# A two-layer hybrid encoder: the middle of the mixer in another order, and two of its masked copies moved from VectorE to ScalarE

## What is computed

```python
def hybrid_layer(x, ...):
    x = x + 0.5 * swiglu_ffn(rms_norm(x, ffn1_norm), ...)
    proj = rms_norm(x, mix_norm) @ w_in
    y_hy = hyena_mixer(hy_in, ...)     # two long convolutions, by DFT
    y_mla = mla_mixer(cq, ckv, kr, ...) # attention, 4 heads, rope on part of q and k
    y_gla = gla_mixer(q, k, v, gf, gb, r, ...) # gated linear attention, both directions
    x = x + concatenate([y_hy, y_mla, y_gla], -1) @ w_out
    return x + 0.5 * swiglu_ffn(rms_norm(x, ffn2_norm), ...)

def mla_mixer(...):
    q = (rms_norm(cq_in, q_norm) @ w_uq).reshape(B, S, MLA_HEADS, dqk)
    q = jnp.concatenate([q[..., :128], rope(q[..., 128:], pos)], axis=-1)
    s = jnp.einsum('bqhd,bkhd->bhqk', q_blk, k) * scale
    p = jax.nn.softmax(s, axis=-1)
    o = jnp.einsum('bhqk,bkhe->bqhe', p, v)      # then rms_norm(o, out_norm)

def gla_chunk_scan(q, k, v, g, inclusive):
    # o[i] = sum over j <= i (j > i in the backward direction) of
    #        (q[i] * exp(sum of g between j and i)) . k[j] * v[j]
```

## Time and profile before

| | |
|---|---|
| median of 3 runs | 1030.2 us (1030.1 to 1030.58) |
| the profiled execution | 1030.28 us |
| its span, first to last instruction | 1028.3 us |
| PE busy | 1001.0 us (97%) |
| DVE busy | 694.3 us (68%) |
| ACT busy | 537.3 us (52%) |
| POOL busy | 110.9 us (11%) |
| mean granted TensorE clock | 0.996 |

### The profile page before, as it was taken

How to read it: one execution, slowest core, us unless ns; L and a number is a source line. 1 busy time by engine, 2 the same in 40 slices (tenths; PEclk the granted TensorE clock), 3 DMA queues, 4 the chain that set the end, 5 groups by cost and what they waited for, 6 DMA issues and landing times.

```text
span 1028.3 us, 14899 instructions
## 1 busy us (share of the span) xinstructions
PE 1001.0 (97%) x5596; PEld 846.5 (82%) x5596; DVE 694.3 (68%) x826; ACT 537.3 (52%) x752; POOL 110.9 (11%) x160
## 2 busy tenths in 40 slices
PE   6999999999899999999999999999998999999997
PEld 5888888888777888888878888887886888888886
DVE  5766656676886666566677665657579776656665
ACT  6554545456654555454465454545466555545453
POOL 2000000150431200000020000003315220000001
PEclk9999999999999999999999999999999999999999
DMA  8466454444303564545455545452542235554551
GB/s 292 170 241 227 165 204 163 164 167 149 136 13 152 177 233 163 204 163 204 165 199 184 225 163 204 163 204 90 198 168 78 83 141 207 184 204 164 203 184 42
DMA packets 27080, 175.85 MB, mean 171 GB/s; under 512 B 3200, under 2 KB 3712, under 8 KB 6560
## 3 DMA queue, kind: packets, MB, share of 16 engines
q1 hardware_dynamic: 25744, 172.90, 45.8%
q0 software_dynamic: 720, 1.95, 0.8%
q10 hardware_dynamic: 576, 0.45, 0.1%
HBM read 174.58 MB, written 1.05 MB: 171 GB/s over the span
## 4 chain that ended last, share of the span: by engine, by line
issue 50%; PE 38%; POOL 9%; DVE 1%; DMA 1%; ACT 1%; POOLq 1%; SPq 0%; ACTq 0%; DVEq 0%
PE psum L1070 16%; PE psum L1071 8%; PE psum L1064 5%; PE psum L1066 4%; PE psum L1065 4%; POOL mixer_scratch L352 3%; POOL mixer_scratch L373 1%; POOL mixer_scratch L372 1%; DMA w_raw<-in_w_dram 1%; POOL statistics L325 1%; POOL statistics L323 1%; POOL x_normed L377 0%; POOL statistics L336 0%; ACT xT_split L430 0%; POOL statistics L339 0%
## 5 line engine op out<-in xcount | busy, mean ns | idle before, releaser
L1070 PE MATMUL psum<-xT_split,w_high 128*128 128x512 f32 x1408 | 501.6, 400 | 4.2 <-DVE w_low L702 2.4
L698 DVE TENSOR_TENSOR w_low<-w_raw,w_high 128x2048 fp32r<-128x2048 f32 (+1 forms) x160 | 362.8, 2270 | 134.4 <-ACT w_high L411 134.4
L1071 PE MATMUL psum<-xT_split,w_low 128*128 128x256 f32 x1408 | 395.6, 281 | 0.0
L1070 PEld LDWEIGHTS psum<-xT_split,w_high 128*128 128x128 f32 x1408 | 265.0, 188 | 72.9 <-issue 6.9
L411 ACT ACTIVATE w_high<-w_raw 128x2048 fp32r<-128x2048 f32 (+1 forms) x160 | 299.7, 1875 | 42.1 <-PE psum L1066 41.5
L1071 PEld LDWEIGHTS psum<-xT_split,w_low 128*128 128x128 f32 x1408 | 266.6, 189 | 1.4
L1064 PE MATMUL psum<-w_high,hT_high 128*128 128x512 f32 (+1 forms) x360 | 140.5, 390 | 0.0
L462 ACT ACTIVATE mixer_scratch<-psum 128x512 f32<-128x512 f32 x88 | 52.5, 596 | 167.4 <-PE psum L1071 167.4
L1066 PE MATMUL psum<-w_high,hT_low 128*128 128x512 f32 (+1 forms) x360 | 139.9, 389 | 0.0
L1065 PE MATMUL psum<-w_low,hT_high 128*128 128x512 f32 (+1 forms) x360 | 139.5, 387 | 0.0
L466 ACT ACTIVATE silu_gate<-hidden 128x256 f32<-128x256 f32 x88 | 36.8, 418 | 135.4 <-DVE hidden L727 135.4
(11 more groups left out here) (187 smaller groups left out, 989.3 us busy)
## 6 DMA issues: line engine op xcount, KB each, us to landing
w_raw<-in_w_dram SPq DMA_DIRECT2D x160, 1024.0 KB, 4.8
w_raw<-in_w_dram SPq DMA_DIRECT2D x8, 256.0 KB, 8.1
x<-in_x_dram SPq DMA_DIRECT2D x2, 512.0 KB, 5.2
mixer_scratch<-in_fil_dram POOLq DMA_DIRECT2D x2, 512.0 KB, 6.1
out_dram<-x_normed SPq DMA_DIRECT2D x3, 256.0 KB, 2.1
mixer_scratch<-in_fil_dram POOLq DMA_DIRECT2D x2, 352.0 KB, 6.1
mixer_scratch<-in_fin_dram SPq DMA_DIRECT2D x1, 512.0 KB, 5.4
dft<-in_dft_dram SPq DMA_DIRECT2D x1, 256.0 KB, 5.1
```

The lines of the kernel that those rows point to most:

```text
L698: e.tensor_tensor(filled(WL[p], n), filled(raw[p], n), filled(WH[p], n).bitcast(F32), ALU.subtract).then_inc(s_lo.sem, 1)
L1070: e.matmul(out, ah, XB[:, k, :, :], start=k == 0, stop=False)
L1071: return e.matmul(out[:, 0:SEQ], al, XH[:, k, :], start=False, stop=k == KD - 1)
```

## The change

Five things change, in both layers; nothing else in the program does.

1. POOL: the rope sum stands ahead of `levels(1)`.
2. PE: the first inverse transform stands ahead of the second query product; the second forward transform ahead of the transposes of the rope sum; heads 2 and 3 of block 1's scores ahead of the second inverse transform, and heads 0 and 1 behind level 1, so that none is left between levels 2 and 3.
3. DVE: `combine` and `fold` of the first convolution come ahead of two weight splits; `gated(0)` ahead of the rope products; `level_qk(3)` ahead of `gated(1)`; the keeps each one place earlier against the products, `level_keep(1)` ahead of `score_max(0)` and `level_keep(3)` ahead of `score_max(1)`.
4. ACT takes over the keeps of levels 5 and 6 as plain copies of square blocks (`blocks_keep`: 4 copies of 32 partitions x 256 elements for level 5, 2 copies of 64 partitions x 512 elements for level 6), and the scaling of the Hyena result (two copies with a scale) that DVE did at L1011.
5. ACT: the copies of the queries, of the odd spectrum and of the keys move by a few places.

```diff
@@ -376,9 +376,9 @@
                 e.wait_ge(q_kt.sem, q_kt.at(l))
                 e.tensor_tensor(xn[:, :, 640:704], KT[:, 0], KT[:, 1], ALU.add).then_inc(q_kr.sem, 1)
                 levels(l, 0)
-                levels(l, 1)
                 e.wait_ge(a_qt.sem, a_qt.at(l))
                 e.tensor_tensor(xn[:, :, 768:1024], PE_[:, 0:2, :], PE_[:, 2:4, :], ALU.add).then_inc(a_qr.sem, 1)
+                levels(l, 1)
                 levels(l, 2)
                 levels(l, 3)
                 rstd(l, h_sq, 2, T_SH, T_RH, I_H, 2, h_r)
@@ -550,6 +550,15 @@
                     r = e.activation(dst, src, ACT.Exp)
                 r.then_inc(g_e.sem, 1)
 
+            def blocks_keep(l, b, bank):
+
+                B = 1 << b
+                e.wait_ge(g_ls.sem, g_ls.at(l, b + 2))
+                for i in range(P // B):
+                    rows_, c = slice(i * B, (i + 1) * B), (i ^ 1) * B
+                    r = e.activation(AD[rows_, :, :, c:c + B], PS[rows_, bank:bank + 4, 0:256].rearrange("p h (t c) -> p h t c", t=T)[:, :, :, c:c + B], ACT.Copy)
+                r.then_inc(g_la.sem, 1)
+
             def probs(l, s):
                 e.wait_ge(a_mx.sem, a_mx.at(l, s + 1))
                 if s:
@@ -632,21 +641,21 @@
                 natural(l, 3, 1, 4)
                 hi(l, S_WO)
                 values_out(1)
+                e.wait_ge(s_used.sem, used(l, S_UQN))
+                for n in range(2):
+                    copy(QN[:, 2 * n:2 * n + 2, :].rearrange("p a b -> p (a b)"), PS[:, 2 + n, :], a_qn)
                 e.wait_ge(a_km.sem, a_km.at(l))
                 copy(KN[:, 0:2, :].rearrange("p a b -> p (a b)"), PS[:, 4, :], a_kn)
                 level_exp(l, 1)
-                e.wait_ge(s_used.sem, used(l, S_UQN))
-                for n in range(2):
-                    copy(QN[:, 2 * n:2 * n + 2, :].rearrange("p a b -> p (a b)"), PS[:, 2 + n, :], a_qn)
                 e.wait_ge(a_vm.sem, a_vm.at(l))
                 copy(VM[:, 0, :], PS[:, 5, :], a_v)
                 copy(VM[:, 1, :], PS[:, 6, :], a_v)
+                spectrum_odd(l, 1, 7)
                 e.wait_ge(a_qtr.sem, a_qtr.at(l))
                 copy(QR.rearrange("p a b -> p (a b)"), PS[:, 2, :], a_qre)
-                spectrum_odd(l, 1, 7)
-                hi(l, S_WO + 1)
                 e.wait_ge(s_used.sem, used(l, S_UKV))
                 copy(KN[:, 2:4, :].rearrange("p a b -> p (a b)"), PS[:, 1, :], a_kn)
+                hi(l, S_WO + 1)
                 level_exp(l, 2)
                 e.wait_ge(g_ls.sem, g_ls.at(l, 1))
                 copy(AD.rearrange("p h t c -> p h (t c)"), PS[:, 0:4, 0:256], g_la)
@@ -659,12 +668,19 @@
                 probs(l, 0)
                 level_exp(l, 5)
                 probs_turned(l, 0)
+                e.wait_ge(h_r.sem, h_r.at(l))
+                for t in range(T):
+                    v = xn[:, t, 0:256]
+                    r = e.activation(v, v, ACT.Copy, scale=st[:, T_RH + t:T_RH + t + 1])
+                r.then_inc(h_yy.sem, 1)
                 level_exp(l, 6)
                 probs(l, 1)
                 turned_high(l, 2, 0, Y_BANKS[0], Y_TILES[0], C_GO, by_parity)
                 probs_turned(l, 1)
+                blocks_keep(l, 5, 0)
                 level_exp(l, 7)
                 attended_squares(0)
+                blocks_keep(l, 6, 4)
                 attended_squares(1)
                 e.wait_ge(g_ls.sem, g_ls.at(l, LEVELS + 1))
                 copy(AC.rearrange("p h t c -> p h (t c)"), PS[:, 4:8, 0:256], g_la)
@@ -974,11 +990,12 @@
                 lo(l, S_UQN)
                 join(l, 0, 0)
                 multiply(l, 0)
-                lo(l, S_UQR)
-                level_qk(l, 0)
-                lo(l, S_UKV)
                 combine(l)
                 fold(l)
+                lo(l, S_UQR)
+                lo(l, S_UKV)
+                level_qk(l, 0)
+                gated(l, 0, 0)
 
                 e.wait_ge(s_used.sem, used(l, S_UQR))
                 q = PS[:, 7, :].rearrange("p (t h d) -> p t h d", t=T, h=H)
@@ -991,7 +1008,6 @@
                 e.tensor_tensor(t1, q, rp(0, 0, 64), ALU.mult)
                 e.tensor_tensor(t2[:, :, :, 0:32], q[:, :, :, 32:64], rp(1, 0, 32), ALU.mult)
                 e.tensor_tensor(t2[:, :, :, 32:64], q[:, :, :, 0:32], rp(1, 32, 64), ALU.mult).then_inc(a_qt.sem, 1)
-                gated(l, 0, 0)
                 lo(l, S_WO)
                 level_qk(l, 1)
                 join(l, 1, 6)
@@ -1000,28 +1016,21 @@
                 fold(l)
                 level_qk(l, 2)
                 level_keep(l, 0)
+                level_qk(l, 3)
                 gated(l, 1, 6)
-                level_qk(l, 3)
+                level_keep(l, 1)
                 score_max(l, 0)
-                level_keep(l, 1)
+                level_keep(l, 2)
                 level_qk(l, 4)
-                e.wait_ge(h_r.sem, h_r.at(l))
-                for t in range(T):
-                    v = xn[:, t, 0:256]
-                    r = e.tensor_scalar(v, v, st[:, T_RH + t:T_RH + t + 1], None, ALU.mult)
-                r.then_inc(h_yy.sem, 1)
-                level_keep(l, 2)
+                level_keep(l, 3)
+                score_max(l, 1)
                 level_qk(l, 5)
-                score_max(l, 1)
-                level_keep(l, 3)
+                level_keep(l, 4)
                 attended(l, 0)
-                level_keep(l, 4)
                 turned_low(l, 2, 0, Y_BANKS[0], Y_TILES[0], C_GO, by_parity)
-                level_keep(l, 5)
                 level_qk(l, 6)
                 attended(l, 1)
                 level_qk(l, 7)
-                level_keep(l, 6, 4)
                 e.wait_ge(a_r.sem, a_r.at(l))
                 for t in range(T):
                     v = xn[:, t, 256:768]
@@ -1339,6 +1348,7 @@
                         r = passes(PS[:, 2 + h // 2, (h % 2) * SEQ:(h % 2 + 1) * SEQ], WH[p][:, k, h * P:(h + 1) * P], WL[p][:, k, h * P:(h + 1) * P],
                                    HH[:, k, :], HL[:, k, :], k == 0, k == 1)
                 r.then_inc(s_used.sem, 1)
+                hy_inverse(l, 0, 0).then_inc(h_inv.sem, 1)
                 e.wait_ge(s_lo.sem, s_lo.at(l, S_UQR + 1))
                 p = pos(S_UQR)
                 for t in range(T):
@@ -1360,18 +1370,18 @@
                     e.wait_ge(g_vr.sem, g_vr.at(l, t + 1))
                     r = passes(PS[:, 5 + t, :], KVH[:, t * P:(t + 1) * P], KVL[:, t * P:(t + 1) * P], WH[p][:, 1, :], WL[p][:, 1, :], True, True)
                 r.then_inc(a_vm.sem, 1)
-                hy_inverse(l, 0, 0).then_inc(h_inv.sem, 1)
                 e.wait_ge(h_oc.sem, h_oc.at(l, 1))
                 keys((2, 3)).then_inc(s_used.sem, 1)
+                e.wait_ge(a_qt.sem, a_qt.at(l))
+                e.wait_ge(a_v.sem, a_v.at(l, 2))
+                e.wait_ge(h_z.sem, h_z.at(l, 1))
+                hy_dft(l, 1, 6)
                 e.wait_ge(a_qr.sem, a_qr.at(l))
                 e.wait_ge(a_qn.sem, a_qn.at(l, 2))
                 for pair in range(2):
                     for t in range(T):
                         r = e.transpose(PS[:, 2, pair * SEQ + t * P:pair * SEQ + (t + 1) * P], xn[:, t, 768 + pair * P:768 + (pair + 1) * P], ident)
                 r.then_inc(a_qtr.sem, 1)
-                e.wait_ge(a_v.sem, a_v.at(l, 2))
-                e.wait_ge(h_z.sem, h_z.at(l, 1))
-                hy_dft(l, 1, 6)
                 e.wait_ge(s_kz.sem, 1)
                 e.wait_ge(a_qre.sem, a_qre.at(l))
                 scores(l, 0, (0, 1))
@@ -1380,13 +1390,14 @@
                 scores(l, 0, (2,))
                 level_scores(l, 0)
                 scores(l, 0, (3,)).then_inc(a_s.sem, 1)
+                e.wait_ge(h_oc.sem, h_oc.at(l, 2))
+                scores(l, 1, (2, 3))
                 hy_inverse(l, 1, 6).then_inc(h_inv.sem, 1)
                 level_scores(l, 1)
                 e.wait_ge(h_z.sem, h_z.at(l, 2))
-                scores(l, 1, (0, 1, 2))
+                scores(l, 1, (0, 1)).then_inc(a_s.sem, 1)
                 level_scores(l, 2)
                 turn_probs(l, 0)
-                scores(l, 1, (3,)).then_inc(a_s.sem, 1)
                 level_scores(l, 3)
                 attend(l, 0)
                 e.wait_ge(h_yy.sem, h_yy.at(l))
```

## The result

| | before | changed |
|---|---|---|
| median | 1030.28 us | 1037.49 us |
| runs | 4, 1030.1 to 1030.58 | 4, 1036.35 to 1039.32 |
| profiled execution | 1030.28 us, span 1028.3 | 1039.32 us, span 1037.2 |
| mean granted clock, profiled | 0.996 | 0.992 |
| PE busy, profiled | 1001.0 us | 1005.0 us |

The ratio of the medians is 1.0071 (95% interval 1.0059 to 1.0083): the change is **slower by 7.2 us**, over three times what a measurement can tell from no change. The forecast was 1034.4 us with a range up to 1037.4: the sign was right, the size too small, and the time lies 0.09 us above the range. The profiled execution is the longest of the changed kernel's four, so a sum made on it comes out larger than one on the medians.

A forecast was written before the change was run, and what follows sets the result against it. PE's work and waits were taken to bound the kernel; 1.53 us for block 1's probabilities plus 0.55 us at the attention's end made 2.1 us per layer, 4.2 us in two: 1034.4 us, range 1030.5 to 1037.4 us.

The forecast's parts named there:

- What bounds the kernel: Whole kernel: time is PE's work (busy 97%), the change can only move PE's waits; clock 1.00 plays no part.
- the main term: probs(1) to turn_probs(1): a chain over PE, VectorE and ScalarE makes block 1's probabilities late, +1.53 us per layer.
- Front: Up to the diagonal's level scores: rope-sum and key waits go, two new ones come; PE 0.3 us early.
- Rival B: A draw: front gains 1 us instead of 0.3, score_max(1) less late; 1030.2 to 1031.6 us; chance 0.15.
- The lock on the rope sum: POOL's sum and VectorE's split exclude each other; split first, sum waits some 2.2 us, costing nothing with 0.3 us cover.
- rival C: Slower: rope sum loses to product behind split, transposes 0.4 us late; level 6 copies 1.5 us; 1036.0 us; chance 0.22.
- The second inverse transform: On PE: two heads fill the 1.55 us wait for fold; start 281.7 instead of 281.96, gaining only 0.25 us.
- Block 0's probabilities: score_max(0) to turn_probs(0): a keep now stands ahead, 0.24 us later; PE waits some 2 us there.
- Block 1's probabilities: Four lists form one chain through level_keep(3); turn_probs(1) starts at 296.64 against 295.11, +1.53 us.
- The end of the attention: Squares stand behind ScalarE's level 6 copies, delaying the transposes of group 1: +0.55 us per layer.
- The block copies: ScalarE's copies outside square blocks, price unknown: level 6's two taken at 1.1 us, bounds 0.75 to 1.5 us.
- The sum: 1.53 + 0.55 = 2.1 us per layer, 4.2 us in two, median 1034.4 us; chance 0.52.

The follow-up runs named there:

- experiment 1: Changed kernel with matmuls repeated in PE's two long waits (block 1's heads 0 and 1, Hyena transposes of group 0), results the same: 1035.85 us.
- experiment 11: Kernel before with only the change's new order up to the first scores, everything behind it as before: 1028.35 us, ratio 0.998.
- experiment 2: Changed kernel with score_max(1) and level_qk(5) ahead of level_keep(3) on VectorE: 1032.65 us, ratio 1.0022.
- experiment 6: Changed kernel with score_max(1) and level_qk(5) ahead of level_keep(3), and attended_squares(1) ahead of level 6's copies: 1030.04 us, ratio 0.9999.
- experiment 9: Kernel before with one line moved on POOL, the rope sum ahead of level 1: 1030.92 us, ratio 1.0001.
- experiment 3: Changed kernel with attended_squares(1) ahead of level 6's copies on ScalarE: 1035.52 us, ratio 1.0045.
- Experiment 5: Changed kernel with the keeps of levels 5 and 6 and the Hyena scaling back on VectorE, new order kept: 1038.12 us, ratio 1.0068.

## Why the prediction was right in sign and too small

**What bounds the kernel: right, with one step that failed.** PE's work and its waits set the time. But "the granted clock is 1.00, so the clock plays no part" read the clock as a property of the stretch, when it is an outcome of the waits. The row was true of the kernel before. The same text forecast waits of 2 us and more, and never asked what the clock does behind a wait longer than any in the earlier trace rows: the clock stood in the sum with nothing. It cost 1.9 us in the medians (experiment 1), and 4.0 us of PE's busy time in the profiled execution. Without it the time would be some 1030.28 + 5.3 = 1035.6 us, an estimate, and inside the range. The rest of the miss, 1.1 us, is size: the main term was taken too small.

**Front.** The first scores start at 275.05 in layer 0. Less the 0.33 us by which the whole layer's mixer starts later in this execution that is 274.72, where 274.45 was forecast: with the 0.38 us wait for keys gone, PE is level with before at the end of the front rather than 0.3 us early. What was missed weighs more: `fold` comes over a microsecond earlier as well, and the front is worth about 1 us per layer if the inverse transform follows at once (experiment 11). Rival B had this number, and was wrong that the change would keep it.

**The lock on the rope sum: right, and free.** POOL's timeline, changed kernel:

```profile
270.01 3.24 POOL L380 TENSOR_TENSOR x_normed<-mixer_scratch 128x512 f32<-128x512 f32 x1 [6.36 <-DVE mixer_scratch L1010]
```

and VectorE's, beside it:

```profile
269.84 2.28 DVE L714 TENSOR_TENSOR w_low<-w_raw,w_high 128x2048 fp32r<-128x2048 f32 x1
272.04 1.76 DVE L853 TENSOR_TENSOR mixer_scratch<-mixer_scratch,silu_gate 128x512 f32<-128x512 f32 x1
```

The sum takes 3.24 us against 1.26, and the split, which is now first, 2.28 us against 3.27: it is the other one that waits now, as forecast. The sum ends at 273.25 us and the transposes start at 273.67 without a wait, so the cover held, and half of rival C falls. It was the 0.68 us product behind the split that lost: beside the sum it took 1.76 us. The Trainium skill, page "SBUF — State Buffer", section "SBUF: two separate sides", says that of a GpSimd operation and a VectorE operation with two SBUF inputs the one that starts first holds the shared port pair for its whole length; these rows agree with it.

**The second inverse transform: nearly right.** 282.25, less the 0.33 us ahead of the stretch, is 281.92, against a forecast of 281.7 and 281.96 before: its wait was filled and nothing gained.

**Block 0's probabilities: mis-sized.** +0.50 us per layer instead of +0.24 (289.62 less 0.33 is 289.29, before 288.79): from `gated(1)` to `score_max(0)` it took 286.19 - 284.18 = 2.01 us, not 1.80. The wait of "some 2 us" was 2.04.

**Block 1's probabilities: the right chain, mis-sized.** Layer 1 is the clean case, since its clock was whole ahead of `turn_probs(1)`. PE's timeline there:

```profile
799.76 1.09 PE L1265 MATMUL psum<-constants,mixer_scratch 128*128 128x128 f32 x8 [2.04 <-ACT mixer_scratch L568]
...
807.60 1.29 PE L1265 MATMUL psum<-constants,mixer_scratch 128*128 128x128 f32 x8 [2.49 <-ACT mixer_scratch L568]
```

From one to the other 7.84 us, against 6.32 before and 7.61 forecast. With the +0.50 the main term is 2.0 us, not 1.53. Nearly all of the 0.23 us lies ahead of `level_keep(3)`: it starts at 801.69, 1.93 us behind `turn_probs(0)`, where the sum had 1.72. The level scores start 1.02 us behind the transposes, not 0.93, and the keep 0.18 us behind their end, not 0.06. In layer 0 the same stretch took 9.23 us, because the half clock lies inside the chain: `level_keep(3)` waits for level scores that were slow themselves.

**The end of the attention: right.** A wait of 0.57 us in layer 0 and 0.58 in layer 1, for 0.55 forecast.

**The block copies: right.** Groups by shape, ScalarE, changed kernel, as the earlier trace rows:

```profile
L559 ACT ACTIVATE mixer_scratch<-psum 32x256 f32<-32x256 f32 x8 | 3.0, 374 | 0.4 <-PE psum L1232 0.4
L559 ACT ACTIVATE mixer_scratch<-psum 64x512 f32<-64x512 f32 x4 | 2.4, 592 | 4.1 <-PE psum L1232 4.1
```

Two copies of level 6 take 1.20 us where 1.1 was taken; the broken access costs nothing, and the other half of rival C falls too. C's time, 1036.0 us, came nearest by luck: both of its reasons were wrong.

**The sum.** Forecast for the order 4.2 us, measured 5.3 (experiment 1) or 4.9 (PE's added idle time), and 1.9 us for the clock on top: 7.2 us. Per layer the order's terms are 0.50 + 1.52 + 0.57 = 2.6 us, against 2.67 in the traces. The profiled execution, 9.04 us longer, closes as 5.3 for the order, 3.4 for the three falls and 0.33 ahead of layer 0's mixer.

**What stays open.** What decides whether the clock falls behind a given wait was not settled: experiments 2 and 6 differ there with the same wait, and so do the two layers of the change's own trace. Over the profiled executions of all fourteen kernels, 13 of the 19 waits of 2.04 to 2.90 us in the mixers' middle were followed by a fall, and 1 of the 9 of 1.55 to 1.64 us; kernels without a wait of 1.5 us there had none. So the length of the wait counts, and something else does too. The split of 7.2 us into 5.3 and 1.9 is one of medians; by their intervals it carries almost 2 us either way, while the traces of single executions show the falls' price directly.

## What to carry to other kernels

A filler moved into one hole of an in-order engine leaves a hole where it was: before moving it, name what will then stand behind the old place, and whether the two holes are equally long and equally late. An operation that waits for an engine's next result must not stand ahead of one that this engine's next step needs; one line (experiment 2) was worth 4.8 us here. And a clock that reads 1.00 before says nothing of the clock after if the change makes the waits longer: price a wait on TensorE with the work behind it at half clock as well, and see whether splitting the wait avoids that.

## What the runs showed that was not expected

- **A fall of the clock has a price of its own, about 1.3 us here.** Three falls in the changed kernel's profiled execution go with 4.0 us more of PE busy time for the same 5596 instructions, 1.3 us each. In experiment 9, falls behind waits of about 2.3 us, one per layer, go with 2.6 us (1003.6 against 1001.0). The time that is lost is somewhat less, 3.4 us for the three, where a later wait takes up a part.
- **Useless work made the kernel faster.** 56 more matmuls in PE's waits took 1.6 us off the median (experiment 1): they held the clock at 1.00 and delayed nothing.
- **It blurs the sum of parts.** Experiments 2 and 3 took 4.8 and 2.0 us off the change, 6.8 in sum; both together took 7.5 off, a difference within the intervals. Experiment 5 took a term of about 1 us away and the median did not move, though its profiled execution, with as many falls, was 1.0 us shorter.
